# One more Strassen unit in a decoder layer: the SSD half of the output projection as seven quarter products

## What is computed

```python
    h = h + jnp.concatenate([y_a, y_b], axis=-1) @ w_out[i]
    hid = jax.nn.relu(rmsnorm(h, norm_mlp_g[i]) @ w_ff1[i])
    h = h + (hid * hid) @ w_ff2[i]
    gate = jax.nn.sigmoid(rmsnorm(h, ple_norm_g[i]) @ w_ple_gate[i])
    h = h + gate * (p[i] @ w_ple_proj[i])
```

## Time and profile before

| | |
|---|---|
| time, median of 3 runs | 725.67 us (725.33 to 726.2) |
| the profiled execution's own time | 725.95 us |
| its span (first to last instruction) | 724.2 us |
| instructions | 9904, of these 3904 matmuls and transposes |
| busy: TensorE, VectorE, ScalarE, GpSimd | 99%, 74%, 58%, 19% |
| HBM read | 98.18 MB |

### The profile page before, as it was taken

How to read it: one execution, slowest core, us unless ns; L and a number is a source line. 1 busy time by engine, 2 the same in 40 slices (tenths; PEclk the granted TensorE clock), 3 DMA queues, 4 the chain that set the end, 5 groups by cost and what they waited for, 6 DMA issues and landing times.

```text
span 724.2 us, 9904 instructions
## 1 busy us (share of the span) xinstructions
PE 715.8 (99%) x3904; PEld 616.1 (85%) x3904; DVE 534.5 (74%) x572; ACT 418.1 (58%) x533; POOL 134.9 (19%) x111
## 2 busy tenths in 40 slices
PE   9999999999999999999999999999999999999996
PEld 7788877888888888888899889988999889988884
DVE  6798784567666465655889975999579957898874
ACT  7754556645665833414776834683358535673885
POOL 1040001765464000001110212121111221020000
PEclk9999999999999999999999999999999999999998
DMA  9932123332431163128867897899887997887311
GB/s 332 314 117 87 59 88 117 117 117 87 164 128 58 63 215 131 56 91 232 206 143 218 184 295 176 218 197 290 168 209 203 250 236 168 214 175 266 112 60 58
DMA packets 53447, 119.83 MB, mean 165 GB/s; under 512 B 5372, under 2 KB 5528, under 8 KB 53400
## 3 DMA queue, kind: packets, MB, share of 16 engines
q1 hardware_dynamic: 40888, 85.60, 34.7%
q0 software_dynamic: 11136, 29.36, 22.3%
q10 hardware_dynamic: 1376, 4.23, 1.7%
HBM read 98.18 MB, written 4.23 MB: 141 GB/s over the span
## 4 chain that ended last, share of the span: by engine, by line
PE 99%; ACT 0%; issue 0%; DVE 0%; ACTq 0%
PE acc L1730 28%; PE acc L1732 28%; PE acc L1731 28%; PE side L1830 3%; PE side L1730 2%; PE side L1731 2%; PE side L1732 2%; PE side L1921 2%; PE side L1888 1%; PE side L1928 1%; PE side L1916 1%; PE acc L1847 1%; PE side L1869 0%; PE side L1868 0%; PE side L1908 0%; PE acc L1739 0%
## 5 line engine op out<-in xcount | busy, mean ns | idle before, releaser
L804 ACT ACTIVATE ring_hi<-quarter 128x1024 fp32r<-128x1024 f32 x112 | 113.6, 1051 | 100.8 <-PE acc L1732 49.5
L1488 DVE TENSOR_TENSOR ring_lo<-quarter,ring_hi 128x1024 fp32r<-128x1024 f32 x112 | 132.8, 1219 | 36.3 <-ACT ring_hi L804 36.1
L1730 PE MATMUL acc<-w_hi,a_hi 128*128 128x512 f32 x252 | 102.7, 407 | 0.0
L1732 PE MATMUL acc<-w_hi,a_lo 128*128 128x512 f32 x252 | 98.4, 391 | 0.0
L1731 PE MATMUL acc<-w_lo,a_hi 128*128 128x512 f32 x252 | 98.2, 390 | 0.0
L662 POOL DMA_DIRECT2D quarter<-in_w_ff x24 | 29.2, 1220 | 235.4 <-DMA quarter<-in_w_ff 235.2
L1731 PE MATMUL acc<-xS_lo,ring_hi 128*128 128x256 f32 x256 | 72.4, 283 | 0.0
L1731 PEld LDWEIGHTS acc<-w_lo,a_hi 128*128 128x128 f32 x252 | 47.4, 188 | 10.9 <-issue 1.7
L1730 PEld LDWEIGHTS acc<-w_hi,a_hi 128*128 128x128 f32 x252 | 47.4, 188 | 10.9 <-issue 1.7
L1732 PEld LDWEIGHTS acc<-w_hi,a_lo 128*128 128x128 f32 x252 | 47.3, 188 | 10.2
L1732 PE MATMUL acc<-xA_hi,ring_lo 128*128 128x256 f32 x192 | 54.3, 283 | 0.0
(11 more groups left out here) (303 smaller groups left out, 1836.3 us busy)
## 6 DMA issues: line engine op xcount, KB each, us to landing
quarter<-in_w_ff SPq DMA_DIRECT2D x72, 512.0 KB, 5.6
w_raw<-in_w_in SPq DMA_DIRECT2D x32, 512.0 KB, 3.6
quarter<-quarter POOLq DMA_DIRECT2D x32, 512.0 KB, 7.9
quarter<-in_w_ff POOLq DMA_DIRECT2D x24, 512.0 KB, 7.8
w_raw<-in_w_out SPq DMA_DIRECT2D x16, 512.0 KB, 3.2
h<-in_x SPq DMA_DIRECT2D x8, 512.0 KB, 5.8
seg<-cs_dram ACTq DMA_DIRECT2D x8, 512.0 KB, 3.8
w_raw<-in_w_ple_gate SPq DMA_DIRECT2D x8, 512.0 KB, 5.1
```

Of the source, the lines that this page charges most:

```text
L804: act.activation(ring[n % 3][0][at], quarter[i][at], ACT.Copy).then_inc(form_hi, 1)
L1488: dve.tensor_tensor(lo[at], src, hi[at].bitcast(F32), ALU.subtract).then_inc(form_lo, 1)
L1730: pe.matmul(dst, st[0], mv[0], start=start, stop=False)
L1732: return pe.matmul(dst, st[1], mv[0], start=False, stop=stop)
```

## The change

Blocks OUT+2 and OUT+3 are gone (`OUT` and `OUT+1` stay; PLE becomes block 11). In their place stand seven products of 512 x 512 quarters, each 24 matmuls (2 token tiles, 4 channel tiles, 3 terms), and additions that put them together in the residual. Left operand: quarters of the turned `y_b`, which now carries 1/rms and the gain. Right operand: quarters of `w_out` rows 1024 to 2047 and sums of them.

- `scale_y`: ScalarE multiplies `y_b` by 1/rms before it is turned (8 instructions, 128x512). The transposes stand after t = 37 to 40.
- `raw_evac`: ScalarE copies each turned bank back into `y` with the gain as scale, in 32 instructions of 128x128, and copies the quarters A11, A12 and A22 to `b_hi`.
- `yb_a_sum`: GpSimd forms S1 = A21-A22, S3 = A21-A11, S2 = A11-S1 and S4 = A12-S2 in place (128x1024 each), behind the transfers of T3, T1 and T2 in its program, each sum waiting for the one before it. ScalarE's `split_sum` waits for all four; VectorE's follows.
- `yb_sum`: eight adding transfers of 512 KB by GpSimd, which make T3, T1, T2 and T4 out of the quarters in `w_raw`. T1 is made in B11's place when B11 has been split, T2 in T1's, T4 in T2's.
- `split_yb`: 14 halves of forms are split, into the places of `w_hi` and `w_lo` that OUT and OUT+1 used.
- `yb_add`: 13 additions on VectorE, each waiting for the one before it.
- The last `turn_norm` stands behind the last PLE group, directly ahead of the feed-forward.
- SyncE's loads of the feed-forward's first quarters come in another order with other waits. Some semaphores are shared with earlier uses.

```diff
-V, X, BC, U, Z, OUT, PLE, GATE = 0, 2, 4, 5, 7, 9, 13, 14
+V, X, BC, U, Z, OUT, PLE, GATE = 0, 2, 4, 5, 7, 9, 11, 12
...
+YB_FORMS = ("B11", "T1", "T2", "T3", "B21", "B22", "T4")
+YB_SLOT = {"B11": 0, "T1": 1, "T2": 2, "T3": 3, "B21": 0, "B22": 2, "T4": 3}
+YB_SUMS = ("S1", "S3", "S2", "S4")
+YB_SPLITS = ("S1", "S2", "S3", "S4")
...
@@ SyncE
-            load_rows(OUT + 2, w_out, 8)
+            load_yb(0, 8, 0, None)
+            load_yb(1, 8, 512, None)
             sp.wait_ge(yb_mul, 8)
             sp.dma_start(tmp[:, 0:2, :], p_dram).then_inc(p_landed, 16)
-            load_rows(OUT + 3, w_out, 12)
+            sp.wait_ge(acc_full, 4 * (OUT + 2))
+            sp.wait_ge(yw_lo, 2)
+            load_yb(0, 12, 0, 0)
+            for p in range(2):
+                sp.wait_ge(ysum_landed[p], 16)
+            load_yb(1, 12, 512, 1)
...
@@ GpSimd
+            for p in range(2):
+                yb_sum(1, 12, 512, p)
+            for p in range(2):
+                yb_sum(0, 8, 512, p, "B11")
+            for p in range(2):
+                yb_sum(0, 12, 512, p, "T1")
...
+            for name in YB_SUMS:
+                yb_a_sum(name)
+            for p in range(2):
+                yb_sum(0, 12, 0, p, "T2")
...
@@ ScalarE
+            for s in range(NS):
+                scale_y(s)
+            for s in range(3):
+                raw_evac(s)
+            split_yb(0)
+            raw_evac(3)
+            split_yb(1)
+            for name in YB_SPLITS:
+                split_sum(name)
+            split_yb(2)
+            split_yb(3)
...
+            ple_evac(0)
+            sums(1, 2)
+            x_evac(0)
+            x_evac(1)
+            ple_evac(1)
+            sums(1, 3)
+            split_form(1, 0)
+            split_form(1, 1)
+            ple_evac(2)
+            x_evac(2)
+            ple_evac(3)
+            x_evac(3)
...
@@ VectorE
+            raw_split(0)
+            raw_split(1)
+            add_group(OUT, 3)
+            raw_split(2)
+            split_yb(0)
+            add_group(OUT + 1, 0)
+            raw_split(3)
+            add_group(OUT + 1, 1)
+            split_yb(1)
+            add_group(OUT + 1, 2)
+            for name in YB_SPLITS:
+                split_sum(name)
+            add_group(OUT + 1, 3)
+            split_yb(2)
+            yb_add("h21 basis")
+            yb_add("h12 basis")
+            yb_add("B11 right")
+            yb_add("B11")
+            split_yb(3)
+            split_yb(4)
...
+            yb_add("T2")
+            yb_add("h12 back")
+            split_yb(5)
+            yb_add("T3")
+            yb_add("h21 back")
+            split_yb(6)
+            yb_add("T1 right")
+            yb_add("T1")
+            yb_add("B21")
+            for p in range(4):
+                split_lo(PLE, p)
+            yb_add("B22")
+            normed(0)
+            normed(1)
+            yb_add("T4")
+            for p in range(2):
+                split_form(0, p)
+            x_evac(0)
+            x_evac(1)
+            normed(2)
+            normed(3)
...
@@ TensorE
+            yb_product("B11", "A11", acc[:, 0:2])
...
+            yb_product("T1", "S1", side[:, 2:4])
+            pe.wait_ge(*emptied(OUT + 1, 3))
+            yb_product("T2", "S2", acc[:, 2:4])
...
+            yb_product("T3", "S3", side[:, 0:2])
+            pe.wait_ge(*added("B11"))
+            yb_product("B21", "A12", acc[:, 0:2])
+            pe.wait_ge(*added("T2"))
+            yb_product("B22", "S4", acc[:, 2:4])
+            pe.wait_ge(*added("T3"))
+            yb_product("T4", "A22", side[:, 0:2])
 
             pe.wait_ge(pt_lo, 2)
-            for s in range(4):
+            pe.wait_ge(*added("B21"))
+            group_pair(PLE, 0, (p_hi, p_lo), 0, nk=2)
+            pe.wait_ge(*added("T4"))
+            turn_norm(1, 0)
+            turn_norm(1, 1)
+            for s in range(1, 4):
                 group_pair(PLE, s, (p_hi, p_lo), 0, nk=2)
-                if s == 1:
-                    turn_norm(1, 3)
+                if s > 1:
+                    turn_norm(1, s)
```

More of the change, by code:

```diff
@@ L110, in build_layer @@
             g_lo = sb("g_lo", [P, KT, SEQ], F32R, where=early)
+        with ExitStack() as early:
+            yb_rows = sb("yb_rows", [P, 2, 4, 512], where=early)
+            ple_rows = sb("ple_rows", [P, 4, 512], where=early)
         x_hi, x_lo, x_raw = {}, {}, {}
@@ L118, in build_layer @@
         x_raw["A21"] = x_raw["S3"]
+        with ExitStack() as early:
+            y_lo = sb("y_lo", [P, NS, D], F32R, where=early)
         x_hi["S1"] = sb("xS1_hi", [P, 4, 256], F32R)
@@ L703, in sums @@
                     if n == 1:
-                        act.wait_ge(*emptied(OUT + 3, s))
+                        act.wait_ge(*added("B22" if s < 2 else "T4"))
                     else:
@@ L802, in split_form @@
                 else:
[L803 removed]
+                    act.wait_ge(*((yb_full, 7) if n < 2 else (acc_full, 4 * (PLE + 1))))
                 act.activation(ring[n % 3][0][at], quarter[i][at], ACT.Copy).then_inc(form_hi, 1)
@@ L996, in _ @@
             yt_evac(0, 2)
             yt_evac(0, 3)
-            for b in range(OUT, OUT + 4):
-                for s in range(4):
[L1000 to L1015, removed]
-                    if b == OUT + 3:
-                        if s >= 2:
-                            x_evac(s - 2)
-                        if s == 3:
-                            for p in range(2):
-                                split_form(0, p)
-                        sums(1, s)
@@ L1025, in _ @@
-            for s in range(4):
-                if s == 0:
-                    x_evac(2)
-                if s == 2:
-                    x_evac(3)
+            split_hi(OUT + 1, 0)
+            yt_evac(1, 0)
+            yt_evac(1, 1)
+            split_hi(OUT + 1, 1)
+            yt_evac(1, 2)
+            yt_evac(1, 3)
+            split_hi(OUT + 1, 2)
+            split_hi(OUT + 1, 3)
+            for s in range(NS):
+                scale_y(s)
+            for s in range(3):
+                raw_evac(s)
@@ new lines, in _ @@
+            split_yb(0)
[5 more added lines that the diff above has]
+            split_yb(3)
+            for k in range(2):
+                act.wait_ge(p_landed, 16)
+                act.activation(p_hi[:, k, :], tmp[:, k, :], ACT.Copy).then_inc(pt_hi, 1)
+            for n in range(4, 7):
+                split_yb(n)
+            for p in range(4):
+                split_hi(PLE, p)
+            sums(1, 0)
@@ L1030, in _, with ple_evac @@
+            sums(1, 1)
+            for p in range(2):
+                split_form(0, p)
+            def ple_evac(s):
                 act.wait_ge(acc_full, 4 * PLE + s + 1)
```

308 lines of the change are left out of this document (227 added, 81 removed).

## The result

The changed kernel takes 735.42 us (median of 4 runs, 733.11 to 736.69) where the kernel before takes 725.93 (4 runs beside it): a ratio of 1.0122, 95% interval 1.0096 to 1.0148, so 9 us slower. Four more runs on another chip gave 733.9 (733.35 to 735.05), ratio 1.0112 (1.0095 to 1.0128). All eight together have a median of 734.3. Forecast were 730.5 and a range to 735.0, both counted from the 725.67 of the kernel before; the ratio of 1.0122 on that is 734.5, though the first median itself lies 0.4 above the range. Two single executions among all those that follow, of 785 and 2537 us, were disturbed and are left out of the medians.

A forecast was written before the change was run, and what follows sets the result against it. TensorE was taken to bound the kernel, with VectorE's dense line binding after the change. -5.4 + 2.5 + 2.2 + 1.5 + 3.7 + 0.3 = +4.8 on 725.95 gave 730.8 profiled, median 730.5 us, range 725.0 to 735.0.

The forecast's parts named there:

- The matmuls: TensorE, changed stage: 192 matmuls become 168, 24 fewer at 0.227 each, 5.44 us less.
- The dense line of VectorE: VectorE bounds without a gap from S1's split at 302.5; 40.8 us to T4's addition at 343.3.
- the products: TensorE waits at T1, T2 and T3, some 0.5, 0.3 and 1.7, entered as 2.5 us.
- the first turn: TensorE at `turn_norm(1, 0)`, which needs T4's bank: a wait of 2.2 us.
- the third norm: Last in VectorE's line behind two form splits and `x_evac`: ready at 352.0, 1.5 us late.
- the tail: Last turn to U takes 26.7 us where TensorE wants 23.0: waits 3.7, half at C11, half at U.
- T3·S3: TensorE's wait at this product, with four additions ahead of its form on VectorE: 1.7 us.
- Four sums ... I take 1.90 plus 0.07: GpSimd's four sums of 128x1024, one after the other: 7.9 us, from 293.4 until 301.3.
- the bound of 2.56: Slower price per GpSimd sum, from a mean of two-tensor operations: four sums end 2.6 us later.
- T1's second transfer: GpSimd's transfer, issued at 281.9, landing 7.8 later at 289.7, with 4.6 and 13.1 kept as extremes.
- T1 lands late or the sums are slow: Rival: T1 takes 10 to 13 us or a sum 2.56; +2.6 to +5, 733 to 736; chance 0.13.
- The clock: Rival: TensorE's clock falls to its lower level at a wait; 733 us; chance 0.07.

The follow-up runs named there:

- The version with both repairs: Changed kernel with the four sums moved to VectorE and the last two norm turns together ahead of the last PLE group: 723.6 us, ratio 0.9968 to the kernel before.
- again: The changed kernel run once more, unedited, on another chip: 733.9 us, ratio 1.0112 to the kernel before.
- T3 apart: Changed kernel with T3's landings counted on semaphores of their own, so T1's second transfer doesn't wait for T3's second landing: 733.7 us, ratio 1.0106.
- same operand: Changed kernel with each GpSimd sum subtracting its left operand from itself, output not the reference's: 733.1 us, one run.
- product for sum: Changed kernel with GpSimd's four sums multiplying instead of subtracting, output not the reference's: 734.3 us, one run.
- second profile: Profiled execution of the changed kernel's unedited second measurement: 733.35 us; that measurement's median is 733.9.
- the tail repaired: Changed kernel with the last two norm turns together ahead of the last PLE group and ScalarE's list reordered: 730.2 us, ratio 1.0062 to the kernel before.
- own sum: Changed kernel with ScalarE's split of S1 waiting for three sums rather than all four: 733.6 us, ratio 1.0096; seven runs of both times have median 733.3.
- the kernel with the sums first: Changed kernel with GpSimd's four sums ahead of T2's two transfers: 732.3 us, ratio 1.0093 to the kernel before.
- first profile: Profiled execution of the changed kernel's first measurement: 736.69 us; that measurement's median is 735.42.
- sums left out: Changed kernel without GpSimd's four sums, the splits taking the quarters as they are: 728.5 us, ratio 1.0037 to the kernel before.

## Why the prediction was right in direction and 4 us short

**The matmuls.** 24 fewer (3904 to 3880), as said. The version with both repairs shows the gain arriving, 2.8 of it.

**The dense line of VectorE.** Forecast: from S1's low half at 302.5 to the T4 product at 383.6, 81.1 us. Five executions that leave this line untouched (changed, again, T3 apart, same operand, product for sum) have 80.93 to 80.96. So with starts from 303.2 to 306.7 every us ahead of the line is a us at the T4 product. It doesn't hold for much earlier starts: the kernels with the same tail that begin the line at 293.8 to 297.8 take 85.1 to 86.3 from there, as other waits come in. Up to the end of T4's addition the forecast had 40.8 (its written terms add up to 40.6); measured are 40.8.

**The waits.** TensorE was to wait 2.5 in the products, 2.2 at the first turn, 1.5 at the third norm, 3.7 at the tail. In the second profile it waits 2.75 (T1), 1.82 (first turn), 1.28 (third norm) and 1.56 + 1.82 = 3.4 (tail). (The T4 product comes 2.2 us later than forecast although these sums are no larger: the low clock in the products is in no wait, and a bracket counts only from the end of a flight.) What should have been split over T1, T2 and T3 came in one, since a long first wait leaves the later ones nothing; where the first is shorter, the wait at T3·S3 is there, 1.46 in the kernels with the tail repaired and with the own sum (forecast 1.7).

**The term that failed: "Four sums ... I take 1.90 plus 0.07".** The mechanism was the forecast's, and this is the term of its sum that was mis-sized: the four took 10.23 and 10.27 where 7.9 stood, 2.35 us more. I had taken the square of one tensor, and the bound of 2.56 was the right row read wrongly: L618 in the earlier trace rows, a mean raised by its longest (3.27); its median in the kernel before is 2.41, and that is the price of two operands read in full. L615, whose second operand is one value per 128 elements, takes 1.90. The first sum of four is 0.47 longer still; it begins before T2's issue has ended (295.38 against 294.62 + 1.19). In the kernel with the sums first no issue runs beside it, and it takes 2.39 like the others; that fits, but no run was made for it. In the experiment with one operand, which has my price, the T4 product starts at 384.13; forecast was 383.6. The Trainium skill (GPSIMD Engine Reference, 3.1 Elementwise), weighed against it in the prediction, gave an estimate of 9.3 us for the four; the trace stands 0.9 above that and 2.35 above mine.

**The rest.** In the second profile: 385.84 - 383.6 = 2.2, all of it the sums, and 733.35 - 730.8 = 2.6; there the sums began at 293.51 where 293.4 was forecast. That is in part luck: T1's second transfer was issued 1.8 us later than I had it (283.65 for 281.9) and landed after 6.5 us instead of 7.8. In the first profile 2.0 more came ahead of the sums: T1's second half landed at 292.0 and not at 289.7 or 290.1. I had missed that its issue waits for T3's landing, and first held this to be the cause; the experiment says that it isn't. A further 1.5 is the clock at the tail. 4.8 + 2.35 + 2.0 + 1.5 = 10.65 against the 10.74 of the first profile (736.69 - 725.95), of which 8.8 lie ahead of the T4 product and 1.9 behind it; the sum comes out this close by chance, as the clock's share is known only roughly. The rival "T1 lands late or the sums are slow" (733 to 736, chance 0.13) is the case that came, by its second half in every run and by its first in one.

**The clock.** I gave it 0.07 and held my waits too short for it. It fell in the first profile at both places. It was 0.52 over 306 to 308, with TensorE still in its wait of 4.34, and 0.51 over 308 to 313, the lower level of 1.2 GHz for nearly all of it, and matmuls started 0.43 apart instead of 0.227. Those 2.3 us cost nothing, since TensorE would have waited for VectorE's dense line anyway: in the kernel with the repaired tail, whose clock stayed 1.00 there, the line from S1's low half to T4's addition takes 39.60 (304.50 to 344.10), as with the fall. Over 385 to 392, behind the waits of 1.56 and 1.82, it was 0.76, and there TensorE sets the end: the rest is 349.0 us. It is 349.0, 348.7 and 349.0 in three others (own sum, sums left out, same operand), which all show this over 380 to 390, as in the kernel with the sums left out:

```profile
380.00:390.00 10.00, 10.00 (x73) 10.00 (x73) 10.00 (x10) 5.63 (x7) 0.00 (x0) 0.83 0.59 177
```

With the same two waits and a clock of 1.00 there it is 347.2 to 348.4. So in 4 of 9 profiles with these waits the clock fell and cost some 1.5 us more (the rests differ by 0.3 to 1.8, and a clock of 0.83 over 10 us is 1.7 us at the full pace), and it fell in none of the three with the repaired tail. The same waits stand in the five profiles without a fall, so what decides it isn't shown. The Trainium skill (TensorE: Matmul & The Clock Gate, HAM oscillation) describes falls to the lower level at waits between bursts, there for transfers; the trace agrees in kind, with waits for other engines.

## What to carry to other kernels

When an algorithm saves the full engine work by adding work to a nearly full second engine, add up that engine's line from the moment it may begin; the average over the stage says little, and a rigid line that starts late passes every further delay ahead of it on in full. Look for a hole of the faster engine for the sums that feed such a line, even when that engine is the busy one: here four sums cost VectorE 5.0 us in a hole and GpSimd 10.2 with 11 us of VectorE's idle time around them. Look for a second loss of its own further on (here the last turn put directly ahead of the feed-forward, 4 to 5 us); only with both repaired did 24 matmuls fewer become 2.5 us less.

## What the runs showed of the hardware

- On GpSimd a two-operand operation of 128x1024 float32 takes 1.90 us when both operands are the same tensor and 2.39 when they are two. VectorE does the same sum in 1.23.
- GpSimd and VectorE take turns when both have only SBUF operands, two on VectorE. In the kernel with the sums first, sums start at 287.57 (2.40), 290.05 (3.26) and 293.39 (3.26) and VectorE's splits at 288.41 (2.64) and 291.0 (3.41). Each split ends 1.1 us behind the sum before it, where it lasts 1.22 alone, and each long sum 2.25 us behind the split, where it lasts 2.39 alone: nothing is shared. VectorE's operation with an operand in PSUM (L1443) takes 1.28 beside them as it does alone. The Trainium skill (SBUF — State Buffer, "SBUF: two separate sides") says this as a rule, an exclusive lock held for the whole instruction; the trace agrees to 0.15 us.
- An adding transfer issued 2 us earlier landed at the same time (8.7 us for 6.5, one profile each).
- The clock fell in or just behind the waits of 4.34, 3.00, 2.75 and 2.62 us at T1·S1 and stayed 1.00 at those of 2.14, 1.61 and 0.98, one profile each. At the tail it fell behind waits of 1.56 and 1.82 in 4 of 9 profiles.
